# A hybrid encoder block: sixteen of the 22 contraction tiles of each down product as seven block products, with weight sums made by adding transfers

## The reference

```python
def swiglu(x, w_gate, w_up, w_down):
    return (jax.nn.silu(x @ w_gate) * (x @ w_up)) @ w_down
...
h = h + 0.5 * rmsnorm(swiglu(rmsnorm(h, pre), w_gate, w_up, w_down), post)   # twice
```

## Time and profile before

| | |
|---|---|
| median of three executions | 1186.32 us |
| profiled execution: time / span from first to last instruction | 1183.95 / 1182.2 us |
| TensorE, VectorE, ScalarE, GpSimd busy | 99%, 69%, 49%, 11% of the span |
| mean granted TensorE clock | 0.996 of full speed (2.4 GHz) |
| down stage of the first block | 238.5 to 359.8 us |
| down stage of the second block | 987.6 to 1108.9 us |

### The profile page before, as it was taken

The page is one execution under the profiler, slowest core; times in us unless marked ns, Lnnn a source line. Parts: engine busy times, 40 slices in busy tenths (PEclk is TensorE's granted clock), DMA queues, the critical chain, the costliest instruction groups (busy, mean ns, idle before and its releaser), DMA issues.

```text
span 1182.2 us, 17769 instructions
## 1 busy us (share of the span) xinstructions
PE 1170.5 (99%) x6860; PEld 1009.6 (85%) x6860; DVE 817.8 (69%) x1309; ACT 582.5 (49%) x921; POOL 131.0 (11%) x111
## 2 busy tenths in 40 slices
PE   9999999999999999999999999999999999999998
PEld 8899999988888886667887888789999998888887
DVE  6888888773337787665466874688888886333574
ACT  6555555533236437666333623565555554323473
POOL 6000000000014000001022201430000000000344
PEclk9999999999999999999999999999999999999998
DMA  6233333342231331111532233322333334232211
GB/s 210 86 107 106 107 107 106 112 138 90 96 93 36 90 107 53 37 38 49 146 89 72 86 111 107 98 81 72 107 106 107 107 106 143 89 106 90 89 37 72
DMA packets 101854, 111.99 MB, mean 95 GB/s; under 512 B 15294, under 2 KB 91678, under 8 KB 101542
## 3 DMA queue, kind: packets, MB, share of 16 engines
q1 hardware_dynamic: 97542, 109.18, 29.8%
q10 hardware_dynamic: 4256, 2.12, 0.6%
HBM read 108.12 MB, written 3.16 MB: 94 GB/s over the span
## 4 chain that ended last, share of the span: by engine, by line
PE 91%; DVE 4%; ACT 3%; issue 2%; DMA 1%; SPq 0%; POOL 0%; ACTq 0%; DVEq 0%
PE bank L303 14%; PE bank L305 14%; PE bank L304 14%; PE bank L781 10%; PE bank L782 10%; PE bank L783 10%; PE bank L626 2%; PE bank L620 2%; PE bank L621 2%; PE bank L310 1%; PE bank L312 1%; PE bank L311 1%; PE bank L1366 1%; PE bank L455 1%; PE bank L1345 1%
## 5 line engine op out<-in xcount | busy, mean ns | idle before, releaser
L337 DVE TENSOR_TENSOR w_lo<-w_raw,w_hi 128x1024 fp32r<-128x1024 f32 x121 | 155.9, 1298 | 173.6 <-ACT w_hi L330 173.3
L330 ACT ACTIVATE w_hi<-w_raw 128x1024 fp32r<-128x1024 f32 x121 | 125.9, 1054 | 191.9 <-PE bank L305 183.1
L781 PE MATMUL bank<-T_hi,w_hi 128*128 128x256 f32 x576 | 163.1, 283 | 1.2 <-ACT bank L1075 1.2
L782 PE MATMUL bank<-T_lo,w_hi 128*128 128x256 f32 x576 | 163.0, 283 | 0.0
L783 PE MATMUL bank<-T_hi,w_lo 128*128 128x256 f32 x576 | 163.0, 283 | 0.0
L303 PE MATMUL bank<-T_hi,w_hi 128*128 128x512 f32 x352 | 137.3, 390 | 0.0
L304 PE MATMUL bank<-T_lo,w_hi 128*128 128x512 f32 x352 | 137.0, 389 | 0.0
L305 PE MATMUL bank<-T_hi,w_lo 128*128 128x512 f32 x352 | 137.0, 389 | 0.0
L303 PE MATMUL bank<-v_hi,w_hi 128*128 128x512 f32 x328 | 132.7, 405 | 0.0
L305 PE MATMUL bank<-v_hi,w_lo 128*128 128x512 f32 x328 | 128.2, 391 | 0.0
L304 PE MATMUL bank<-v_lo,w_hi 128*128 128x512 f32 x328 | 127.8, 390 | 0.0
(11 more groups left out here) (311 smaller groups left out, 2333.5 us busy)
## 6 DMA issues: line engine op xcount, KB each, us to landing
w_raw<-in_ffn_w_up SPq DMA_DIRECT2D x44, 512.0 KB, 4.0
w_raw<-in_ffn_w_down SPq DMA_DIRECT2D x44, 512.0 KB, 3.5
w_raw<-in_ffn_w_gate SPq DMA_DIRECT2D x43, 512.0 KB, 4.0
w_raw<-in_w_in SPq DMA_DIRECT2D x32, 512.0 KB, 3.7
w_raw<-in_w_out SPq DMA_DIRECT2D x8, 512.0 KB, 3.4
w_raw<-in_ple_w_gate SPq DMA_DIRECT2D x8, 512.0 KB, 3.4
x_tm<-in_x SPq DMA_DIRECT2D x4, 512.0 KB, 7.6
Mb<-m_rows ACTq DMA_DIRECT2D x8, 256.0 KB, 4.9
```

The source lines that it names most:

```text
L330: nc.scalar.activation(w_hi[:, s, :], w_raw[:, s, :], ACT.Copy).then_inc(w_hi_done, 1)
L337: nc.vector.tensor_tensor(w_lo[:, s, :], w_raw[:, s, :], w_hi[:, s, :].bitcast(F32), ALU.subtract).then_inc(w_lo_done, 1)
L781: nc.tensor.matmul(o, whi, a_hi(kk), start=(start and kk == 0), stop=False, skip_group_check=True)
L782: nc.tensor.matmul(o, whi, a_lo(kk), start=False, stop=False, skip_group_check=True)
```

## The change

Tiles 0 to 15 of the contraction are taken as two halves of eight tiles, the 1024 outputs as two halves of 512, the tokens as two halves of 256. Seven products of half by half by half (`down_product`, 4 chunks by 4 output tiles by 6 matmuls of 256 columns each) with sums of blocks replace eight. Partial results move between banks: ScalarE copies four tiles after products 0, 2 and 4 (`down_copy_act`), VectorE adds four after products 3 and 4 (`down_seed_dve`). Four matmuls of 512 columns open the upper banks. The two operands of a product that are sums of activations are made by VectorE (`down_raw_dve`), rounded by ScalarE (`down_hi_act`) and subtracted by VectorE (`down_lo_dve`), in halves a = 0, 1 of 1024 columns; products 2, 3, 4 and 6 (the third, fourth, fifth and seventh) have such sums.

Weight sums are made in memory by transfers: SyncE loads a first block into `sum_a` or `sum_b`, which lie where `v_hi` and `v_lo` were, and GpSimd issues transfers that add another block to it (`accum_op`). Products 2, 3 and 5 take their weights from three successive states of `sum_a`, product 4 from `sum_b`. Tiles 16 to 21 stay conventional and come last; the first 512 columns of their weights are negated when they are split, and the norm's gain takes the sign back. The down stage now has 34 chunks (DNN) instead of 22, and 42 transfers of 512 KB, 16 of them adding.

```diff
+SK = 16
+DNN = 28 + KF - SK
...
+    sum_a = at("sum_a", [P, 4, 2, 512], F32, cursor[0])
     v_hi = sb("v_hi", [P, KD, S], F32R)
+    sum_b = at("sum_b", [P, 4, 2, 512], F32, cursor[0])
     v_lo = sb("v_lo", [P, KD, S], F32R)
...
+    negated = {m + j for m in (DN1 + 28, DN2 + 28) for j in range(KF - SK)}
...
+        src = w_raw[:, s, :]
+        if n in summed:
+            src, made, value = summed[n]
+            act.wait_ge(made, value)
+        else:
+            act.wait_ge(w_loaded[s], LOADED[n])
...
+        if n in negated:
+            nc.scalar.activation(w_hi[:, s, 0:512], src[:, 0:512], ACT.Copy, scale=-1.0)
+            src = src[:, 512:1024]
+            nc.scalar.activation(w_hi[:, s, 512:1024], src, ACT.Copy).then_inc(w_hi_done, 1)
+            return
...
+        def product_done(eng, p, m):
+
+            if m < 3:
+                own.wait(eng, "mm", MM0 + 3 * p + m + 1)
+            else:
+                eng.wait_ge(w_used, DN + 4 * p + 4)
+
+        def down_operand(tile, p):
+
+            return tile[:, 2 * (p % 2):2 * (p % 2) + 2, :, :].rearrange("p a k c -> p (a k) c")
+
+        def block_rows(k0, row):
+
+            c = 512 * (1 - row)
+            return wd[0, k0 * P:(k0 + 2) * P, c:c + 512].rearrange("(k p) c -> p k c", p=P)
+
+        for c in range(4):
+            chunk = lambda t: t[:, c, :, :].rearrange("p k c -> p (k c)")
+            for e in range(4):
+                src = chunk(sum_b if e == 2 else sum_a)
+                summed[DN + 8 + 4 * e + c] = (src, own[f"sum{c}"], own.before(f"sum{c}") + 16 * (e + 1))
...
+            def rows_loaded(n, k0, row, then):
+
+                if n < DN + 4:
+                    qd = QUADS - 2 + (n - DN) // 2
                     own.wait(sp, "s_dve", 4 * qd + 4)
                     own.wait(sp, "s_lo", 4 * qd + 4)
                 else:
-                    sp.wait_ge(w_lo_done, m - RING + 1)
-                sp.dma_start(w_raw[:, m % RING, :], wd[0, k * P:k * P + P, :]).then_inc(w_loaded[m % RING], 16)
+                    sp.wait_ge(w_lo_done, then + 1)
+                sp.dma_start(w_raw[:, n % RING, :].rearrange("p (k c) -> p k c", k=2), block_rows(k0, row)).then_inc(w_loaded[n % RING], 16)
+
+            for c in range(4):
+                rows_loaded(DN + c, 2 * c, 0, None)
+            own.wait(sp, "mm", 7 * (QUADS - 1) + 6)
+            for c in range(4):
+                sp.dma_start(sum_a[:, c, :, :], block_rows(2 * c, 1)).then_inc(part_in[c], 16)
+            for c in range(4):
+                rows_loaded(DN + 4 + c, SK // 2 + 2 * c, 0, DN + c)
+            for c in range(4):
+                sp.dma_start(sum_b[:, c, :, :], block_rows(2 * c, 0)).then_inc(consts_in, 16)
+            for c in range(4):
+                rows_loaded(DN + 24 + c, SK // 2 + 2 * c, 1, DN + 4 + c)
+            for j in range(KF - SK):
+                m = CONVENTIONAL + j
+                sp.wait_ge(w_lo_done, m - RING + 1)
+                sp.dma_start(w_raw[:, m % RING, :], wd[0, (SK + j) * P:(SK + j + 1) * P, :]).then_inc(w_loaded[m % RING], 16)
...
-            def down(k, j, first=False):
-                pe.wait_ge(w_lo_done, k + (DN + 1))
-                own.wait(pe, "plo", k + 1)
+            def down_product(p, left, upper, first=False):
+
+                a_hi, a_lo = down_operand(T_hi, p), down_operand(T_lo, p)
+                for c in range(4):
+                    nw = DN + 4 * p + c
+                    pe.wait_ge(w_lo_done, nw + 1)
+                    if c % 2 == 0:
+                        own.wait(pe, "t_lo", 4 + 2 * p + c // 2 + 1)
+                    for m in range(4):
+                        if first and c == 2 and m == 3:
+                            own.wait(pe, "post", POST1)
+                            for u in range(4, 8):
+                                nc.tensor.matmul(B[YBANK[u]][:], wv(nw, 0, P)[0], a_hi[:, 0:2, :].rearrange("p k c -> p (k c)"),
+                                                 start=True, stop=True)
+                        if c == 0:
+                            if p == 0 and m == 0:
+                                own.wait(pe, "post", POST1 - 4)
+                            if p == 1:
+                                own.wait(pe, "rcopy", COPY0 + m + 1)
+                            if p == 3:
+                                own.wait(pe, "rcopy", COPY0 + 4 + m + 1)
+                            if p == 4:
+                                own.wait(pe, "post", POST1 + m + 1)
+                            if p == 6:
+                                own.wait(pe, "post", POST1 + 4 + m + 1)
+                        o = B[YBANK[m + 4 if upper else m]][:, 0:256] if left else B[YBANK[m + 4 if upper else m]][:, 256:512]
+                        for kk in range(2):
+                            k = 2 * c + kk
+                            whi, wlo = wv(nw, kk * 512 + m * P, kk * 512 + (m + 1) * P)
+                            start = first and k == 0
+                            nc.tensor.matmul(o, whi, a_hi[:, k, :], start=start, stop=False, skip_group_check=True)
+                            nc.tensor.matmul(o, whi, a_lo[:, k, :], start=False, stop=False, skip_group_check=True)
+                            last = nc.tensor.matmul(o, wlo, a_hi[:, k, :], start=False, stop=(k == 7), skip_group_check=True)
+                        if m == 3:
+                            last.then_inc(w_used, 1)
+                        elif c == 3:
+                            last.then_inc(own["mm"], 1)
+
+            down_product(0, False, False, first=True)
+            down_product(1, True, True)
+            down_product(2, True, False)
+            down_product(3, False, False)
+            down_product(4, False, False)
+            down_product(5, False, True)
+            down_product(6, True, False)
+
+            for j in range(4):
+                pe.wait_ge(w_lo_done, CONVENTIONAL + j + 1)
+                own.wait(pe, "t_lo", 18 + j + 1)
                 for m in range(KD):
-                    if first and m in (0, 4):
-                        own.wait(pe, "post", POST0 + 4 * (QUADS - 1 + m // 4))
-                    last = three(B[YBANK[m]][:], wv(DN + j, m * P, (m + 1) * P), split_slot(T_hi, j), split_slot(T_lo, j),
-                                 first, False)
+                    last = three(B[YBANK[m]][:], wv(CONVENTIONAL + j, m * P, (m + 1) * P), split_slot(T_hi, SK + j),
+                                 split_slot(T_lo, SK + j), False, False, skip_group_check=True)
                 last.then_inc(w_used, 1)
...
+        t12 = wsum[:].rearrange("p a k c -> p (a k c)").rearrange("p (k c) -> p k c", c=256)
+        t3 = scratch[:].rearrange("p a c -> p (a c)").rearrange("p (k c) -> p k c", c=256)
...
+        def down_source(p, a):
...
+            k = slice(4 * a, 4 * a + 4)
+            if p in (0, 1, 5):
+                k0 = (0 if p == 0 else SK // 2) + 4 * a
+                return prod[:, k0:k0 + 4, (256 if p == 5 else 0):(512 if p == 5 else 256)]
+            return (t3 if p == 4 else t12)[:, k, :]
...
+        def down_raw_dve(dve, p, a):
...
+            k = slice(4 * a, 4 * a + 4)
+            lo, up = slice(4 * a, 4 * a + 4), slice(SK // 2 + 4 * a, SK // 2 + 4 * a + 4)
+            o = down_source(p, a)
+            if p == 2:
+                own.wait(dve, "s_lo", 4 * (QUADS - 1) + 3)
+                ins = nc.vector.tensor_tensor(o, prod[:, lo, 0:256], prod[:, lo, 256:512], ALU.subtract)
+            elif p == 4:
+                own.wait(dve, "prod_ready", NI)
+                ins = nc.vector.tensor_tensor(o, prod[:, up, 256:512], prod[:, lo, 256:512], ALU.subtract)
             else:
...
+                own.wait(dve, "t_lo", 4 + 2 * (p - 1 if p == 3 else 3) + a + 1)
+                c = slice(256, 512) if p == 3 else slice(0, 256)
+                ins = nc.vector.scalar_tensor_tensor(o, o, -1.0, prod[:, up, c], ALU.mult, ALU.subtract)
+            ins.then_inc(own["t_raw"], 1)
...
+        def down_hi_act(act, p, a):
+
+            if p in RAWS:
+                own.wait(act, "t_raw", RAWS[p] + a + 1)
+            else:
+                own.wait(act, "prod_ready", SK // 2)
+            if p < 2:
+                own.wait(act, "mm", 7 * (QUADS - 1) + 3 if p == 0 else MM0)
+            else:
+                act.wait_ge(w_used, DN + 4 * (p - 1))
+            nc.scalar.activation(down_operand(T_hi, p)[:, 4 * a:4 * a + 4, :], down_source(p, a), ACT.Copy).then_inc(own["t_hi"], 1)
...
+        def down_lo_dve(dve, p, a):
+            own.wait(dve, "t_hi", 4 + 2 * p + a + 1)
+            k = slice(4 * a, 4 * a + 4)
+            nc.vector.tensor_tensor(down_operand(T_lo, p)[:, k, :], down_source(p, a), down_operand(T_hi, p)[:, k, :].bitcast(F32),
+                                    ALU.subtract).then_inc(own["t_lo"], 1)
...
+        def down_copy_act(act, p, m):
+
+            product_done(act, p, m)
+            left, right = B[YBANK[m]][:, 0:256], B[YBANK[m]][:, 256:512]
+            if p == 0:
```

(71 more changed lines are left out.)

104 lines of the change are left out of this document (58 added, 46 removed).

## The result

The changed kernel took **1206.86 us** (median of 4 runs, 1206.0 to 1207.27) against 1185.40 (4 runs, 1183.57 to 1186.39) before: ratio 1.0182, interval 1.0170 to 1.0195. It is 21.5 us slower; the forecast was 12.7 us slower, 1199.0, with a range of 1184 to 1222. The profiled execution took 1207.27 us with a span of 1205.4 and a mean granted clock of 0.985 (0.996 before).

What follows compares the result with a forecast made beforehand. TensorE, busy 99% of the span, bounds the kernel. Per FFN 80.6 + 0.9 + 0.35 + 6.6 (late load) + 4.9 (pace) = 93.4 us against 87.0; twice, +12.7 us: 1199.0 us, range 1184 to 1222.

Steps and rivals of the forecast that it cites:

- Matmuls: Down stage, per FFN: 256-column matmuls keep 0.120 us; 80.6 + 0.9 us replace 87.0, gaining 5.5 us.
- Rival 4: Products: 256-column matmuls outside a loop take 0.127 us, not 0.120; 4.7 us more per FFN, +9.4; chance 0.05.
- the start: First product: the 1024-column operand subtraction ends at 238.83, TensorE wants it at 238.49; a wait of 0.35 us.
- Third load of the second product: Additions beside it delay its landing to 17.9 us of the stage; TensorE then waits 6.6 us before the second product.
- my two contended ends: Third load's landing beside additions: 15.3 us if sharing evenly at load price, 20.4 if additions cost twice and take two thirds.
- the 4 us that I took: Start of the stage: GpSimd's additions run beside the loads from about 4 us.
- Pace of the engines: ScalarE and VectorE taking turns need 12.3 us per product against TensorE's 11.5, in three successive products.
- The waits of 1.4 and 3.3 us: TensorE waits 1.4 us for ScalarE's copies before the fourth product, 3.3 for VectorE's adds before the fifth; together 4.7.
- Price of an addition: An adding transfer of 512 KB costs the DMA engines between 1.36 us, like a load, and twice that.
- Rival 3: Additions at 4 us or more each leave the fourth and fifth product waiting for weights; +38 us, 1224; chance 0.15.
- Later additions hide: Twelve later additions, 1.36 to 2.7 us each, have about 10 us each from issue to need, so cause no wait.
- My sign of a full queue: Down stage: queue share near 1.0 from 4 to 20 us of the stage.

Runs made afterwards that it cites:

- e2: The change with GpSimd's first four additions per FFN cut to 16 columns (does not compute the layer): 1188.8 us, ratio 1.003.
- e5: The change with VectorE making each operand difference one product earlier: 1194.6 us, ratio 1.007.
- e8: The change's own transfers; operand differences one product earlier, ScalarE's copies before the second product's third split, VectorE's four adds earlier: 1195.7 us, ratio 1.008.
- e3: The change with GpSimd's first additions issued only once ScalarE has rounded the second product's last chunk: 1201.3 us, ratio 1.013.
- e6: The change with first additions waiting for the second product's last load, and loads of sum_b and the seventh product issued later: 1203.0 us, ratio 1.014.
- e7: e6 plus operand differences made one product earlier and VectorE's four adds put before the second half of the fifth's operand: 1198.2 us, ratio 1.012.
- e9: e7 with GpSimd's first additions starting on the second product's second load instead of its fourth: 1193.6 us, ratio 1.006.
- e10: e7 with the fifth product's sums left out, sum_b zeroed and its additions cut to 16 columns (does not compute the layer): 1179.0 us, ratio 0.994.
- e12: e11 with ScalarE's four copies put ahead of the split of the second product's third tile: 1180.85 us, ratio 0.9976.
- e1: The change with GpSimd's sixteen transfers per FFN copying instead of adding (does not compute the layer): 1199.8 us, ratio 1.011.
- e11: e7 with sum_b added on VectorE without transfers, and GpSimd's first additions starting on the second product's third load: 1184.1 us, ratio 0.9987.

## Why the prediction was right, and where its sum was short

Direction, mechanism and place were right; the size was 9 us short of the measured 21.5. Step by step:

- **Matmuls.** Distance of 256-column starts in straight code: 0.120 us, as taken. Rival 4 is out. The four opening matmuls took 0.93 us (starts from 247.27 to 248.20) against 0.9, the start 0.42 against 0.35.
- **Third load of the second product**: landing forecast at 17.9 us of the stage; its split began at 257.00 - 238.86 = 18.1 (238.86 is where the first product would have started without its own wait). The wait: forecast 6.6, 6.69 in the first FFN. e2 shows that the cause is the right one. That the middle of my two contended ends was right on the spot is in part luck: the splits that follow loads stand 3.94 and 4.07 us apart in ScalarE's rows, which is the pace of my upper end (three times 1.36, 4.1), not of the middle (3.4); but by that pace and the landing the additions began to press on the loads about 1 us later than the 4 us that I took (an estimate). In the second FFN the wait was 8.30: there the second product's first split already began 1.6 us later in the stage (11.7 against 10.1), and the next two followed at the same pace.
- **Pace of the engines**: forecast 12.3 us per product. VectorE's first half operand of the third, fourth and fifth product:

```profile
263.18 1.22 DVE L1082 TENSOR_TENSOR wsum<-prod 128x1024 f32<-128x1024 f32 x1
...
275.46 1.22 DVE L1089 SCALAR_TENSOR_TENSOR wsum<-wsum,prod 128x1024 f32<-128x1024 f32 x1
...
287.73 1.22 DVE L1085 TENSOR_TENSOR scratch<-prod 128x1024 f32<-128x1024 f32 x1
...
298.87 1.42 DVE L1132 TENSOR_TENSOR bank<-bank,T_raw 128x256 f32<-128x256 f32 x4
```

  12.3 us apart, and the three-operand form costs what the plain one does (1.22). The waits of 1.4 and 3.3 us are 1.36 and 3.15 (1.81 and 3.15 in the second FFN). e5 removed the first and more than half of the second by order alone, so their reason holds too.
- **Price of an addition**: bounds 1.36 and 2.7 us for 512 KB; measured 2.57 where only additions run. Rival 3 (4 us and more) is out.
- **"Later additions hide"** is the step that was right for a reason I did not see. In the change TensorE never waits for a sum, as I wrote; but it seems only since its other waits gave the additions the time: in e5 and e8, whose engines keep ahead, ScalarE waits for sums of the fourth product before its splits, up to 1.65 and 3.89 us. I compared each addition with its own 10 us and never added up the engines' time over the stage, 47.2 us in some 47 to 56. My sign of a full queue "from 4 to 20 us" of the stage was wrong: it is full until 62. This is why e3, e6 and e7 won little (6, 4 and 9 us).
- **The step that failed: the granted clock**, which I left at full. Behind the waits it went to 0.50. In the products that cost 3.3 + 3.0 us. In the stretch after the first FFN another 1.8 came, where 18 matmuls of 128 columns took 3.68 us in place of 2.25. TensorE's row there, and two stretches (granted clock third from the end):

```profile
371.16 3.68 PE L514 MATMUL bank<-ident 128*128 128x128 f32 x18
...
370.00:372.00 2.00, 2.00 (x18) 2.00 (x18) 1.05 (x4) 1.61 (x4) 0.00 (x0) 0.93 0.00 0
372.00:374.00 2.00, 2.00 (x12) 2.00 (x11) 1.60 (x4) 0.68 (x1) 0.00 (x0) 0.50 0.00 0
```

That last fall is not behind a wait and may not be the change's: it came 68 us after the one before, and the profiled executions of e7, e8, e9, e10 and e12 have one at this place as well, those of e1 to e6 and e11 none.

The profiled executions differ by 1207.27 - 1183.95 = 23.3 us. Forecast 12.7, clock in the products 6.3, clock behind the first FFN 1.8, the second FFN's longer wait 1.7: 22.5. The other 0.8 us is spread over pieces of under 0.5 us.

The Trainium skill (DMA: Bandwidth & Descriptors, Queues, rings and completion order) has each engine serve its queues in turn, packet by packet. The runs agree: with GpSimd's additions beside them the second and third load let ScalarE go 3.94 and 4.07 us after the one before, which is the time of one load and one addition (1.36 + 2.57 = 3.93), and loads landed at up to 17.8 us from issue. Without those additions (e2) the second followed the first after 1.33 us.

What the profiles of the change and the twelve kernels show of the clock is this. In the products TensorE waited over 0.45 us 66 times. Behind the 34 waits of up to 2.96 us the granted clock stayed at 1.00. Of the 11 between 3.14 and 3.32 us nine were followed by a fall to 0.50 (all of the change's, e1's and e2's, not e11's 3.15), and so were all 21 of 3.38 us and more. The loss behind one fall does not grow with the wait: 1.5 us in e2 behind 3.15, 1.5 and 1.9 in e5 behind 7.57 and 9.89, and 2.5 and 2.7 in e1 behind 5.24 and 3.16. Two waits of 3.15, the stretch behind the one in e2 (granted clock 0.68 on the mean, 23 matmuls) and in e11 (1.00, 32 matmuls):

```profile
292.00:296.00 4.00, 3.88 (x23) 3.91 (x24) 2.09 (x4) 0.00 (x0) 0.00 (x0) 0.68 0.88 161
...
254.60:258.60 4.00, 3.89 (x32) 3.92 (x33) 4.00 (x4) 2.70 (x5) 3.99 (x4) 1.00 0.76 121
```

So the change paid four times for four waits, and e5 twice. What decides near 3.2 us, and between a loss of 1.4 and one of 2.7, stays open; a kernel that keeps TensorE busy through the wait wasn't tried.

## What to carry to other kernels

Where a change turns evenly spaced loads into bursts and sums, add up the DMA engines' time over the whole stage, with each kind of transfer at its own rate, and compare it with the time in which the stage needs them; if it comes near 1, do not expect much of reordering (seven tries here won 4 to 13 of the 21.5 us, and none got below the kernel before), and let an engine that idles make a sum of two tiles that are both on the chip. A saving in matmul slots of a few per cent is gone at the first wait, and a wait of over 3 us cost more than its length here (1.4 to 2.7 us behind 30 of 32 such waits), since the clock fell behind it: price it. And look at what stands in front of a short instruction on an in-order engine (here four copies behind a split whose load is late).

## What the runs showed of the hardware

- A transfer that adds moves 202 to 206 GB/s at full share of the 16 engines, one that copies 384: 2.57 against 1.36 us for 512 KB. GpSimd spends 1.20 us to issue one.
- In the changed kernel additions of 512 KB landed 5.7 to 16.8 us after their issue, depending on what else was queued, and beside loads one addition passed for each load (about 4 us the pair); the same engine share (1.1) moves 261 GB/s where loads and additions mix.
- The granted clock fell to 0.50 behind waits of 3.1 to 9.9 us and behind none of up to 2.96, and 256-column matmuls then stood 0.213 us apart (0.120 at full clock) for some 3 to 6 us. Kernels with short waits vary with it from run to run: e11 took 1179.9 us at 0.997 and 1187.3 at 0.989.
- VectorE kept 1.22 us for a subtraction of 128x1024 in two-input form beside full queues of GpSimd's additions.
